# Sums of chunks and of squares on GpSimd ahead of the ones-products, and moved steps around the heads

## The reference, cut to what matters

```python
h = mlstm_chunkwise(q, k, v, i_pre, logf)          # per head
h = jax.nn.sigmoid(heads(z).astype(f32)) * h       # the gate
mu = jnp.mean(h, axis=-1, keepdims=True)
var = jnp.mean(jnp.square(h - mu), axis=-1, keepdims=True)
h = ((h - mu) * lax.rsqrt(var + EPS)).reshape(bsz, seq, MLSTM_WIDTH)
h = h * mh_gain.astype(f32) + skip.astype(f32) * xc.astype(f32)
return h.astype(xm.dtype) @ w_proj
```

## Time and profile before

| | us |
|---|---|
| median of 3 executions | 4072.47 (4071.83 to 4073.72) |
| the profiled execution | 4072.61 |
| its span | 4071.1 |
| PE busy in it | 3991.0 |
| DVE busy | 2476.5 |
| ACT busy | 1230.7 |
| POOL busy | 968.6 |

### The profile page before, as it was taken

How to read it: one execution, slowest core, us unless ns; L and a number is a source line. 1 busy time by engine, 2 the same in 40 slices (tenths; PEclk the granted TensorE clock), 3 DMA queues, 4 the chain that set the end, 5 groups by cost and what they waited for, 6 DMA issues and landing times.

```text
span 4071.1 us, 53758 instructions
## 1 busy us (share of the span) xinstructions
PE 3991.0 (98%) x19149; PEld 3445.9 (85%) x19149; DVE 2476.5 (61%) x3435; ACT 1230.7 (30%) x1301; POOL 968.6 (24%) x690
## 2 busy tenths in 40 slices
PE   8999999998999999999999999999999999999998
PEld 5887777776788788888888888888899999999997
DVE  7556877467533654545766663222247888888885
ACT  4333223334223322222333332222222222222222
POOL 1100000323111445454000000000024444444432
PEclk9999999999999999999999999999999999999999
DMA  4533333652543454546777778666768888888883
GB/s 174 196 138 129 117 126 121 212 172 98 178 144 131 156 176 164 175 165 202 245 239 237 241 240 310 218 219 214 228 222 301 318 308 311 316 313 316 304 318 133
DMA packets 239906, 867.73 MB, mean 213 GB/s; under 512 B 22584, under 2 KB 61000, under 8 KB 172128
## 3 DMA queue, kind: packets, MB, share of 16 engines
q1 hardware_dynamic: 96576, 454.07, 30.5%
q10 hardware_dynamic: 94080, 204.49, 16.3%
q0 software_dynamic: 49184, 208.36, 14.7%
HBM read 768.25 MB, written 232.81 MB: 246 GB/s over the span
## 4 chain that ended last, share of the span: by engine, by line
PE 64%; DVE 6%; DMA 3%; issue 3%; POOL 2%; ACT 1%; DVEq 0%; SPq 0%; ACTq 0%; POOLq 0%
PE mm L1961 15%; PE mm L1962 15%; PE mm L1963 15%; PE pv L1961 3%; PE pv L1962 2%; PE pv L1963 2%; DMA raw<-stream 2%; PE sc L1961 2%; PE sc L1962 2%; PE sc L1963 2%; DVE wlo L1136 2%; POOL el L647 1%; DVE acc L1885 1%; PE st L1963 1%; PE st L1962 1%
## 5 line engine op out<-in xcount | busy, mean ns | idle before, releaser
L1136 DVE TENSOR_TENSOR wlo<-raw,whi 128x2048 fp32r<-128x2048 f32 x329 | 755.9, 2299 | 760.2 <-ACT whi L695 737.8
L695 ACT ACTIVATE whi<-raw 128x2048 fp32r<-128x2048 f32 x378 | 724.1, 1916 | 505.7 <-issue 217.2
L1961 PE MATMUL mm<-t_hi,whi 128*128 128x512 f32 x2048 | 801.0, 391 | 6.4 <-DVE t_lo L1690 3.2
L1962 PE MATMUL mm<-t_lo,whi 128*128 128x512 f32 x2048 | 799.1, 390 | 0.0
L1963 PE MATMUL mm<-t_hi,wlo 128*128 128x512 f32 x2048 | 798.8, 390 | 0.0
L1961 PEld LDWEIGHTS mm<-t_hi,whi 128*128 128x128 f32 x2048 | 385.6, 188 | 89.7 <-DVE t_lo L1690 6.0
L1963 PEld LDWEIGHTS mm<-t_hi,wlo 128*128 128x128 f32 x2048 | 385.5, 188 | 80.9
L1962 PEld LDWEIGHTS mm<-t_lo,whi 128*128 128x128 f32 x2048 | 385.8, 188 | 77.7
L1961 PE MATMUL mm<-hn_hi,whi 128*128 128x512 f32 x960 | 377.4, 393 | 4.8 <-DVE wlo L1136 4.8
L1962 PE MATMUL mm<-hn_lo,whi 128*128 128x512 f32 x960 | 374.2, 390 | 0.0
L1963 PE MATMUL mm<-hn_hi,wlo 128*128 128x512 f32 x960 | 373.8, 389 | 0.0
(11 more groups left out here) (438 smaller groups left out, 7264.3 us busy)
## 6 DMA issues: line engine op xcount, KB each, us to landing
raw<-stream SPq DMA_DIRECT2D x380, 1024.0 KB
ev_d<-stream ACTq DMA_DIRECT2D x128, 1024.0 KB, 6.2
up_d<-sgl ACTq DMA_DIRECT2D x128, 256.0 KB, 2.1
g_d<-gst ACTq DMA_DIRECT2D x12, 2048.0 KB, 11.5
gg<-g_d SPq DMA_DIRECT2D x15, 1536.0 KB
gl<-up_d SPq DMA_DIRECT2D x120, 192.0 KB
spill<-stage ACTq DMA_DIRECT2D x44, 256.0 KB, 2.0
xm_d<-xms POOLq DMA_DIRECT2D x12, 512.0 KB, 5.4
```

Source lines behind the costliest of these rows:

```text
L695: act.activation(whi[:, k, :], raw[:, k, :], ACT.Copy).then_inc(hi_done, 1)
L1136: dve.tensor_tensor(wlo[:, k, :], raw[:, k, :], whi[:, k, :].bitcast(F32), ALU.subtract)\
L1961: pe.matmul(out, lh, rh, start=start, stop=False)
L1962: pe.matmul(out, lh, rl, start=False, stop=False)
```

## The change

For heads 0 to 2 GpSimd's `z_gate` adds the three gated chunks into `sz[:, 0, :]`, and a new `square_sum` adds the three squares into the first of them; TensorE's `mean_of_sum` and `squares_of_sum` multiply each sum by ones once. They stand later: the mean behind `scores(0)`, the squares between the weighted values of chunks 1 and 2. The load of `sz` for the next head waits for the mean (`mu_done`). VectorE takes over `finished_low`, the gates of head 3 and the odd chunks of `t_lo` in the second norm. Its order within a head changes: two low parts of the next head's q come ahead of the `gh` chunks, one of them ahead of the reciprocal; `scale` moves from the end of a head into the next one; skips, centre and variance stand later. The variance has its own buffer (`hs2` in place of `rd`), and ScalarE's order follows. Behind the last head the order changes as well. `xm` of head 0 is loaded ahead of the last GLU block. In the second norm the first query's scaling goes behind all chunks (on ScalarE `first_query` too). In the first down group the third unit is loaded ahead of `gg`, and VectorE's first weight split stands ahead of the wait for `gg`. The last store is cut into two. The diff, cut to its core:

```diff
@@ -341,10 +341,11 @@
...
                 for v in range(8):
-                    if g or v != 1:
+                    if g or v not in (1, 2):
                         load_down(g, v)
...
                         load_down(0, 1)
+                        load_down(0, 2)
                     if v == 0:
@@ -365,8 +366,9 @@
...
             store(finp_done, FIN_V + 3, KC, KC - FIN_V)
-            store(fin_done, 8, FIN_V, FIN_V)
-            sp.wait_ge(fin_out, 16 * 5)
+            store(fin_done, 8, FIN_V - 1, FIN_V - 1)
+            store(fin_done, FIN_V - 1, FIN_V, FIN_V)
+            sp.wait_ge(fin_out, 16 * 6)
@@ -472,8 +474,16 @@
...
+            def next_xm(h):
+                pool.wait_ge(proj_done, O_QKV + 10 * h)
+                pool.dma_start(xm_hi[:], xm_heads[h, 0]).then_inc(xm_in, 16)
+                pool.dma_start(xm_lo[:], xm_heads[h, 1]).then_inc(xm_in, 16)
             for p in range(KC // 2):
                 for b in range(2):
+                    if p == KC // 2 - 1 and b == 1:
+                        next_xm(0)
                     glu_block(p, b)
@@ -489,6 +499,16 @@
...
                     pool.tensor_tensor(gh[:, c, :], gh[:, c, :], sz[:, c, :], ALU.mult).then_inc(hz_done, 1)
+                    if c:
+                        pool.wait_ge(hz_done, 5 * h + 2 * c)
+                        pool.tensor_tensor(sz[:, 0, :], sz[:, 0, :] if c > 1 else gh[:, 0, :], gh[:, c, :], ALU.add)\
+                            .then_inc(hz_done, 1)
+            def square_sum(h):
+                for c in range(1, HC):
+                    pool.wait_ge(hsq_done, 5 * h + 2 + c)
+                    pool.tensor_tensor(hsq[0], hsq[0], hsq[c], ALU.add).then_inc(hsq_done, 1)
@@ -497,19 +517,6 @@
...
                                        xc_lo[:, 3 * h + c, :].bitcast(F32), ALU.add).then_inc(xs_done, 1)
-            def finished_low(h):
...
-            def next_xm(h):
...
@@ -520,13 +527,12 @@
...
-                pool.wait_ge(hz_done, 3 * h)
+                pool.wait_ge(mu_done, h)
...
-            next_xm(0)
             load_conv(1, slice(MC - HC - 1, MC))
@@ -536,13 +542,11 @@
...
                     skips(h - 2, (2,))
-                    finished_low(h - 2)
                 if h < HEADS - 1:
                     next_xm(h + 1)
+                square_sum(h - 1)
                 skips(h - 1, (0, 1))
-            z_gate(HEADS - 1)
             skips(HEADS - 2, (2,))
-            finished_low(HEADS - 2)
             skips(HEADS - 1, range(HC))
@@ -589,10 +593,6 @@
...
             pool.dma_start(h2_d, h2[:]).then_inc(h2_copied, 16)
-            for d in range(1, KC, 2):
-                pool.wait_ge(ahi_done, 3 * KC + d + 1)
-                pool.tensor_tensor(t_lo[:, d, :], xt[:, 1, :], t_hi[:, d, :].bitcast(F32), ALU.subtract)\
-                    .then_inc(alo_done[1], 1)
             pool.wait_ge(khi_done, 1)
@@ -854,25 +854,27 @@
...
                 weights(0)
+                qkv(5)
                 weights(1)
-                qkv(5)
+                qkv(6)
+                weighted_high(0)
                 if h >= 2:
-                    tail_high(h - 2, hh)
-                qkv(6)
+                    tail_high(h - 2, hh, range(2))
+                qkv(7)
+                weights(2)
+                weighted_high(1)
+                if h >= 2:
+                    tail_high(h - 2, hh, range(2, HC))
+                qkv(8)
+                weights(3)
                 if h:
                     tail_squares(h - 1, hh)
-                weighted_high(0)
-                qkv(7)
-                weights(2)
-                if h:
-                    tail_root(h - 1)
-                weighted_high(1)
-                qkv(8)
-                weights(3)
                 weighted_high(2)
...
                 weighted_high(3)
+                if h:
+                    tail_root(h - 1)
                 split_hi(U_QKV // 2 + h + 1, 1)
@@ -886,9 +888,9 @@
...
             spare_hi(1, pv_done, MC)
-            tail_high(HEADS - 2, hh)
             tail_squares(HEADS - 1, gh)
             tail_root(HEADS - 1)
+            tail_high(HEADS - 2, hh)
             tail_high(HEADS - 1, gh)
@@ -1501,12 +1503,19 @@
...
                 dve.wait_ge(var_done, h + 1)
-                dve.tensor_scalar(rd[:], dn[:], 1.0 / HD, EPS, ALU.mult, ALU.add).then_inc(msd_done, 1)
+                dve.tensor_scalar(hs2[:], dn[:], 1.0 / HD, EPS, ALU.mult, ALU.add).then_inc(msd_done, 1)
...
+            def finished_low(h, buf):
+                for c in range(HC):
+                    dve.wait_ge(hfhi_done, 3 * h + c + 1)
+                    dve.tensor_tensor(xc_lo[:, 3 * h + c, :], buf[:, c, :], xc_hi[:, 3 * h + c, :].bitcast(F32),
+                                      ALU.subtract).then_inc(hflo_done, 1)
@@ -1555,51 +1564,54 @@
...
-                for j in range(1 if h else 0, 4):
+                for j in range(2 if h else 0, 5):
                     qkv(h, j)
+                dve.wait_ge(bcst_in, 32 * h + 48)
+                exponent(0)
+                qkv(h, 5)
+                exponent(1)
                 if h >= 2:
+                    scale(one, h - 2)
                     gain(one, h - 2, hh)
+                qkv(h, 6)
+                weighted(0)
+                if h >= 2:
                     skip(h - 2, 0, hh)
                     skip(h - 2, 1, hh)
-                dve.wait_ge(bcst_in, 32 * h + 48)
-                exponent(0)
-                qkv(h, 4)
-                exponent(1)
-                if h >= 2:
-                    skip(h - 2, 2, hh)
-                qkv(h, 5)
-                if h:
-                    dve.wait_ge(hflo_done, 3 * (h - 1))
-                    centre(h - 1, hh)
-                qkv(h, 6)
-                weighted(0)
                 exponent(2)
...
                 qkv(h, 7)
-                if h:
-                    variance(h - 1)
                 weighted(1)
+                if h >= 2:
+                    skip(h - 2, 2, hh)
                 exponent(3)
                 weighted_low(1)
+                if h >= 2:
+                    finished_low(h - 2, hh)
+                    dve.wait_ge(hflo_done, 3 * (h - 1))
+                if h:
+                    centre(h - 1, hh)
                 qkv(h, 8)
...
                 weighted(3)
+                if h:
+                    variance(h - 1)
                 weighted_low(3)
...
                 split_lo(U_QKV // 2 + h + 1, 1)
-                if h:
-                    scale(one, h - 1)
...
                 one(dve.tensor_tensor(rd[:], dn[:], rd[:], ALU.max))
+                if h < HEADS - 1:
+                    qkv(h + 1, 0)
                 one(dve.reciprocal(rd[:], rd[:]))
                 if h < HEADS - 1:
-                    qkv(h + 1, 0)
+                    qkv(h + 1, 1)
                 for c in range(HC):
@@ -1615,24 +1627,23 @@
...
+            for c in range(HC):
+                dve.wait_ge(pv_free, MC - HC + c + 1)
+                dve.tensor_tensor(gh[:, c, :], gh[:, c, :], sz[:, c, :], ALU.mult).then_inc(hz_done, 1)
             spare_lo(0)
+            scale(one, HEADS - 2)
+            centre(HEADS - 1, gh)
+            spare_lo(1)
             gain(one, HEADS - 2, hh)
+            variance(HEADS - 1)
             for c in range(HC):
                 skip(HEADS - 2, c, hh)
-            dve.wait_ge(pv_done, MC)
-            spare_lo(1)
-            centre(HEADS - 1, gh)
-            variance(HEADS - 1)
+            finished_low(HEADS - 2, hh)
             scale(one, HEADS - 1)
...
                 skip(HEADS - 1, c, gh)
-            dve.wait_ge(hflo_done, MC - HC)
...
+            finished_low(HEADS - 1, gh)
@@ -1684,8 +1695,6 @@
...
             def norm_low(d):
-                if d % 2:
-                    return
                 dve.wait_ge(ahi_done, 3 * KC + d + 1)
@@ -1711,16 +1720,14 @@
...
             next_lo(U_HEAD // 2, 1)
-            first_scaled(0)
-            for d in range(4, 12):
-                normed(d)
-            first_low(0)
-            for d in range(12, KC):
+            for d in range(4, KC):
                 normed(d)
...
             next_lo(U_HEAD // 2 + 1, 0)
-            first_scaled(1)
-            first_low(1)
+            for k in range(2):
+                first_scaled(k)
+            for k in range(2):
+                first_low(k)
@@ -1894,12 +1901,14 @@
...
             def down_group(g, slots, peeled=False):
-                dve.wait_ge(gn_in, 16 * g + 16)
                 if slots:
+                    dve.wait_ge(gn_in, 16 * g + 16)
                     weights(BATCH * (g - 1), BATCH, BATCH * g)
...
                     down_lo(g, v)
+                    if v == 0 and not slots:
+                        dve.wait_ge(gn_in, 16 * g + 16)
                     dve.wait_ge(upn_in[v % 2], 64 * g + 16 * (v // 2) + 16)
@@ -2074,19 +2083,29 @@
...
+            def mean_of_sum(h):
+                pe.wait_ge(hz_done, 5 * h + 5)
```

(33 more changed lines are left out.)

17 lines of the change are left out of this document (3 added, 14 removed).

## The result

The changed kernel takes 4052.2 us (median of 5 runs, 4046.1 to 4053.3) against 4072.5 for the kernel before in the same session (5 runs). The ratio is 0.9946, with a 95% interval of 0.9933 to 0.9959, so it is faster by 0.54%. The profiled execution took 4049.6 us with a span of 4048.0, against 4072.6 and 4071.1: 23.1 us less.

The account below looks back on a forecast made before the run. TensorE, busy 98% of the span, was taken as the bound, with VectorE setting the heads' period. Gains of 3.5 + 4.0 + 6.0 + 5.3 + 7.5 + 0 = 26.3 us from 4072.6, less 0.1, gave 4046.2 us; range 4037 to 4060.

Parts of the forecast that it names:

- parts 1, 3: Heads: dropped ones-products save 10.3 us of TensorE's work, but VectorE sets the period; 3.5 us won over three heads.
- the 42.9 of the sum: VectorE's chain added up around one late head: 42.9 us against 43.4 before, 0.5 us a head.
- VectorE takes back what TensorE is given: Heads 1 to 3: VectorE's chain sets the period once TensorE's waits go, leaving 0.5 us a late head.
- part 2: Shared SBUF ports: a VectorE instruction on SBUF alone waits for GpSimd's running one, up to 1.25 us.
- part 4: Head 0: earlier xm load removes TensorE's wait and half clock; 4.0 us won, ends 1.5 and 4.8.
- part 5: First to last group of merged products: VectorE's reordered chain takes 36.3 us, 6.0 less; ends 3 and 7.5.
- part 6: Second norm: all low chunks on VectorE let TensorE go on 5.3 us sooner, half clock staying about as long.
- part 7: Down stage start: split ahead of the wait for gg and earlier third-unit load win 7.5 us; ends 4 and 8.2.
- No wait at the down start: Down stage start: TensorE would show no wait there after the change, where 8.1 us were lost before.
- part 8: End of the kernel: cutting the last store in two brings 0, between -0.5 and 0.5 us.
- TensorE sets the heads' period: Rival, heads: VectorE finds gaps between GpSimd's steps, three heads gain 9 to 10 us, total 4040; chance 0.14.
- GpSimd's sums starve VectorE: Rival, heads: all ten GpSimd steps hold VectorE's chain, a head takes 52.2 us, total 4076; chance 0.04.

Follow-up runs that it names:

- no_sums: Changed kernel without GpSimd's twelve additions: mean and variance of heads 0 to 2 take three ones-products each again; 4050.9 us, ratio 0.9947.
- idle_sums: Changed kernel with three ones-products each for mean and squares, GpSimd's additions kept but waited for by nobody, six with unread sums; 4050.5 us, ratio 0.9946.
- no_square_sum: Changed kernel with the mean summed on GpSimd but the squares added up by three ones-products; 4048.3 us, ratio 0.9944.
- best2: Changed kernel without mean and square sums, xm transfers apart, low halves ahead of third skip, four tiles for the skips' GpSimd sums; 4049.7 us, ratio 0.9945.
- only_sums: Kernel before plus GpSimd's twelve additions and the single ones-products alone, in the old order of all engines' lists; 4089.1 us, ratio 1.0042.

## Why the prediction was right, and where it was not

The forecast of 4046.2 had the sign and most of the size: 26.3 us less, of which the traces show 23.1 and the medians 20.3. By its own parts:

- **Ones-products (parts 1, 3).** 48 records became 24, and the heads changed by 3.7 us where 3.5 was taken. Heads 2 and 3 take 42.6 and 41.6 us for the 42.9 of the sum. The sentence "VectorE takes back what TensorE is given" is borne out by `no_sums` and was still too kind: up to the first merged product the sums take 3 to 4 us more than they give, though behind the heads that evens out. What made the heads shorter was the order, 7.8 us, which the prediction did not price apart from the sums. That the total came out at 3.7 is partly luck: `exponent(0)` was 1.7 us too dear in the sum, the product of the squares with its hand-offs took 2.2 and 1.7 us (from the end of the additions to `variance`) where 1.1 was put, and the lower clock behind TensorE's wait was not thought of. Head 1 gained 0.9 where nothing was forecast; its wait for `k_lo` was 0.50 and not 2.1.
- **Ports (part 2).** The `exponent(0)` of 2.6 us took 0.93: it ends at 951.46, while GpSimd's next multiply runs (951.13 to 952.61), so VectorE does get turns between GpSimd's steps. In `idle_sums` GpSimd's additions beside VectorE cost about 1 us over three heads.
- **`xm` (part 4).** -2.8 for -4.0. The step that failed is that `ya_d` would come perhaps 1.5 us late and be hidden until `k_lo`. VectorE waited 3.44 us for it and began its first low half 8.9 us behind the start of head 0, where it was 6.05 before: 2.9 us late. TensorE waited 1.33 for `q_lo`:

```profile
830.86 0.61 POOL L469 DMA_DIRECT2D ya_d<-vt  x1 [0.30 <-POOL vt L467]
...
836.16 1.29 DVE L1536 TENSOR_TENSOR q_lo<-mm,q_hi 128x512 fp32r<-128x512 f32 x2 [3.44 <-DMA ya_d<-vt]
...
836.91 0.50 PE L1970 MATMUL mm<-xc_hi,whi 128*128 128x512 f32 x1 [1.33 <-DVE q_lo L1536]
```

- **Behind the heads (part 5).** 36.8 us for the 36.3 that the addition of VectorE's list gave, and again partly luck. The weight splits ended with the first merged product (980.40) and not 2.0 us behind it, and VectorE's list then took about 2 us longer than the sum, mostly in two waits of 1.2 us for GpSimd's sums and in the low halves of head 2 (4.0 us for 2.5). Nor is it the last low half that decides: TensorE waits 4.43 us for the low halves of head 2 and then needs 10.6 us for its own products, at a mean clock of 0.77, before the last group.
- **Second norm (part 6).** -7.0 for -5.3. The order gave what was forecast: the first query unit starts 17.5 us behind the third unit, where it was 22.7. The assumption that half clock would stay is what failed: the other 1.8 us are the clock's.
- **Start of the down stage (part 7).** -6.7 for -7.5, and 1.8 given back over the next four units, so 4.9 net. "No wait at the down start" did not hold: VectorE gates the unit before with a gathered row that it waits 5.93 us for, the split of the third unit stands behind that, and TensorE waits 1.49 us. The fourth unit was named as late next and then not priced. In this trace it comes in time and the fifth is late; in `idle_sums` and `no_square_sum` it is the fourth (3.4 and 3.0 us).

```profile
2961.51 0.56 DVE L1867 TENSOR_TENSOR gl<-gl,gg 128x384 f32<-128x384 f32 x1 [5.93 <-DMA gl<-up_d]
...
2985.34 0.43 PE L1970 MATMUL pv<-actb,whi 128*128 x1 [1.38 <-DVE wlo L1138]
```

- **Last store (part 8).** From 4040 to 4046 the DMA engines are as full as in the earlier trace rows (share 1.01 for 1.02); a gain of half a microsecond is below the spread of the stage.

Of the rivals, "TensorE sets the heads' period" falls with `no_sums`. "GpSimd's sums starve VectorE" put a head at 52.2 us; the changed kernel is far from it. The old order with the sums comes to 50.8, but not by that mechanism: VectorE is idle 35.5 us of its three heads, against 25.2 in the kernel before, and what fills the head are TensorE's waits for the sums, 10.7 us in head 2. The size was real, the reason was another, and the new order is what kept it away.

## What to carry to other kernels

Work taken from the busiest engine is no gain if the replacement ends in a chain that the same engine waits for: ask when the result is ready, not what the step costs. Try an offload in the old order and in the new one, and the new order without the offload; only the four together tell which of them earned the time. Two errors of opposite sign can give the right total, so a stage that agrees with the forecast does not yet prove the reason given for it.

## What the hardware showed that was not expected

- An addition of GpSimd holds up VectorE's work on SBUF where the two meet without a gap: 0.69 us became 1.77 and 1.66 in `best2`. This agrees with the Trainium skill (SBUF — State Buffer, section SBUF: two separate sides), by which the two share a port pair that one of them holds for its whole instruction. But VectorE got its turn between two of GpSimd's steps, so ten steps a head cost far less than ten blocked instructions (about 1 us over three heads in `idle_sums`).
- Behind the wait of 3.97 us for the squares in head 2 TensorE's granted clock was 0.50 for 3.2 us, and over heads 1 to 3 it was 0.96 in the changed kernel and 0.91 in `only_sums`; in the kernel before, in `no_sums` and in `idle_sums` it was 1.00. The wait is not all that a late sum costs.
- The granted clock of the same 12 us of the norm, with the same code in it, was 0.50, 0.57 or 0.86, and the time followed it (1.2 us between the ends). TensorE had waits of up to 1.0 us between its products ahead of that stretch. With the shorter list of VectorE they were 0.4 to 0.8 us, and the clock was 1.00 in nine traces of nine. What decides between 0.50 and 0.86 in the same code stays open.
- The down stage from its third unit on took 1079 to 1088 us in 14 traces. The four kernels with its old start had 1079.3 to 1083.1 (mean 1080.8), the ten with a new one 1081.0 to 1088.2 (mean 1083.9). Most of that difference is the loss over the four units behind the start, 0.4 to 6.1 us: from the seventh unit on, both sorts take 1045.9 to 1049.9. So the changed start keeps on average some 4 of its 7 us, and the changed kernel's +0.1 in the ledger is 1.8 lost and 1.7 of that spread.
